# The order of the high and low weight products in the four feed-forwards of a two-block transformer kernel

## The chip, the core and the metric

The kernel runs on one core of one Trainium2 chip. Its time is the device time of one execution, in microseconds (us). The kernel before takes 1095.96 us, the median of three executions from 1095.06 to 1097.74 us.

## What is computed

Two transformer blocks run one behind the other on one sequence of 256 tokens of width 1024, in float32. The first is feed-forward, sparse attention with a pooling branch, feed-forward; the second is feed-forward, a gated mixer, feed-forward. The four feed-forwards are the places that the change is about (the gated mixer is touched as well). Cut to them:

```python
D_MODEL = 1024
SEQ = 256
D_FF = 2816

def swiglu(x, w_gate, w_up, w_down):
    return (jax.nn.silu(x @ w_gate) * (x @ w_up)) @ w_down

x = x + 0.5 * swiglu(rms_norm(x, ffn1_norm[l]), ffn1_w_gate[l], ffn1_w_up[l], ffn1_w_down[l])
...
z = h @ w_in                      # the gated mixer's first projection, width 7168
y_a = spatial_gating(u, v, sgu_norm, sgu_w, sgu_b) @ w_proj_a
y_b = (gate_b * short_conv(gate_c * xb, conv_w)) @ w_proj_b
```

## The kernel before

**Split numbers.** Each float32 operand is held as the sum of a high and a low part in the type fp32r. The activations lie side by side in one tile, `x_hl[:, k, 0, :]` high and `x_hl[:, k, 1, :]` low, 256 tokens each; `hid_hl`, `ya_hl` and `yb_hl` are the same for the hidden features and the mixer's branches. A product of a 128x128 weight tile takes two passes of TensorE into one PSUM bank of 512 columns. The **high pass** (`w_hi` as weights) streams 512 columns, high and low activations at once. The **low pass** (`w_lo` as weights) streams the 256 high columns and is added to the bank's first half. The product of low with low is left out. Each pass loads its own 128x128 weights. A high pass and a low pass of one tile are called a pair below.

**Weights.** They come from memory as blocks of 128x1024, eight 128x128 tiles each, in the order of use, through a ring of four slots (`RING`). SyncE issues the transfers, ScalarE rounds a block into `w_hi` (L429), VectorE subtracts to get `w_lo` (L780) and raises `w_split`. TensorE waits for `w_split` at the first pass of a block and raises `w_used` at its last, which frees the slot.

**A feed-forward** (`ffn(e, n0, p)`, e from 0 to 3) has 66 blocks. `wide_block` takes one block, eight pairs for k = 0 to 7 (`KC`), into one bank. The first two blocks are worked in turn with each other (k outside, two banks), the next two by `wide_block`; then `sum_squares` adds the squares for the norm (L1321); then come 40 blocks, a gate and an up block for each of the 20 remaining chunks of 128 hidden features, the last 32 of them in a hardware loop. For a chunk ScalarE and VectorE make the hidden features, and GpSimd subtracts the high part from them (L347) and raises `hid_split`, once for each of the 22 chunks (`FC`). The down part is 8 output tiles m of 22 pairs k. The weight tile of m and k is number 22m+k in a row of blocks of eight, so the 22 pairs of an m are cut at the ends of blocks: 8, 8 and 6 for m = 0. In m = 0 each k waits for its own chunk (`hid_split`).

**The gated mixer** calls `wide_block` for 56 blocks. The attention mixer does not: it works by `three`, three passes of equal length (L1250 to L1252). No planner sets an order: each engine's program is written out, and semaphores hold the engines together.

Of the kernel before, what the change touches and what calls it, by code (L numbers as in the profile page):

```python
# [26 lines left out]
P = 128  # L27
D = 1024
S = 256
KC = D // P  # L30
TT = S // P
FF = 2816
FC = FF // P
# [13 lines left out]
RING = 4  # L47
# [7 lines left out]
UP_B = 2 * FC  # L55
# [21 lines left out]
def build(nc, stream, x_in, cols_in, rows_in, const_in, sgu_w_in, pool_w_in, out):  # L77
    ctx = ExitStack()
    with ctx:
# [41 lines left out]
        hid_hl, mix_hl, ya_hl, yb_hl = wide[:, 0:FC], wide[:, 0:KC], wide[:, KC:2 * KC], wide[:, 2 * KC:3 * KC]  # L121
# [50 lines left out]
        bank = [pair[i // 2][:, i % 2, :] for i in range(8)]  # L172
# [45 lines left out]
        hid_split = sem("hid_split")  # L218
# [1028 lines left out]
        def _(pe):  # L1247
            def three(dst, a_hi, a_lo, b_hi, b_lo, first, last):
# [2 lines left out]
                nc.tensor.matmul(dst, a_hi, b_lo, start=False, stop=False, skip_group_check=True)  # L1251
                return nc.tensor.matmul(dst, a_lo, b_hi, start=False, stop=last, skip_group_check=True)  # L1252

            def both(dst, a_hi, a_lo, b_hl, first, last):

                nc.tensor.matmul(dst, a_hi, b_hl.rearrange("p a s -> p (a s)"), start=first, stop=False, skip_group_check=True)  # L1256
                return nc.tensor.matmul(dst[:, 0:S], a_lo, b_hl[:, 0, :], start=False, stop=last, skip_group_check=True)  # L1257

            def wide_block(n, dst, b_hl, i=0, per=0):

                slot = n % RING
                pe.wait_ge(w_split, n + 1 + per * i)
                for k in range(KC):
                    w = slice(k * P, (k + 1) * P)
                    last = both(dst[:], w_hi[:, slot, w], w_lo[:, slot, w], b_hl[:, k, :, :], k == 0, k == KC - 1)
                last.then_inc(w_used, 1)

            def feature_block(n, dst, b_hi, b_lo, i=0, per=0, p=None, ready=None):
# [61 lines left out]
            def ffn(e, n0, p):  # L1330

                if p == 0:
                    pe.wait_ge(half_split, 2)
                for k in range(KC):
                    if k == (KC // 2 if p == 0 else 0):
                        pe.wait_ge(w_split, n0 + 2)
                    pe.wait_ge(x_split, 8 * p + k + 1)
                    w = slice(k * P, (k + 1) * P)
                    for c in range(2):
                        slot = (n0 + c) % RING  # L1340
                        last = both(bank[4 + c][:, :], w_hi[:, slot, w], w_lo[:, slot, w], x_hl[:, k, :, :], k == 0, k == KC - 1)
                        if k == KC - 1:
                            last.then_inc(w_used, 1)
                wide_block(n0 + 2, bank[6], x_hl)
                wide_block(n0 + 3, bank[7], x_hl)
                sum_squares(p)

                def chunk(f, j, i=0):

                    wide_block(n0 + 2 * f, bank[2 * j], x_hl, i, 8)  # L1350
                    wide_block(n0 + 2 * f + 1, bank[2 * j + 1], x_hl, i, 8)
# [12 lines left out]
                for m in range(KC):  # L1364
                    if m == 0:
                        pe.wait_ge(parts_added, FC * e + FC - 3)
                    elif m == 2:
                        pe.wait_ge(parts_added, FC * e + FC - 2)
                    elif m >= 4:
                        pe.wait_ge(down_read, KC * e + m - 3)  # L1370
                    for k in range(FC):
                        tile = FC * m + k
                        n, w = n0 + UP_B + tile // KC, slice(tile % KC * P, (tile % KC + 1) * P)
                        if tile % KC == 0:
                            pe.wait_ge(w_split, n + 1)
                        if m == 0:
                            pe.wait_ge(hid_split, FC * e + k + 1)
                        last = both(bank[m % 4][:, :], w_hi[:, n % RING, w], w_lo[:, n % RING, w], hid_hl[:, k, :, :], k == 0,
                                    k == FC - 1)
                        if tile % KC == KC - 1:  # L1380
                            last.then_inc(w_used, 1)
                        elif k == FC - 1:
                            last.then_inc(down_done, 1)

            def attention_mixer(n0, p):
# [202 lines left out]
MIX1_SPLITS = (1, 2, 4, 7, 9)  # L1588

DOWN_LAST = [((m + 1) * FC - 1) // KC for m in range(KC)]  # L1590
DOWN_ENDS = [((m + 1) * FC) % KC == 0 for m in range(KC)]

STAT = [3, 3, 3, 3, 3, 3, 4]
# [109 lines left out]
```

## Time and profile before

| what | us |
|---|---|
| time, median of three executions | 1095.96 |
| the profiled execution's own time | 1094.97 |
| its span in the trace | 1093.2 |
| TensorE busy (share of the span) | 1080.8 (99%) |
| VectorE busy | 783.8 (72%) |
| ScalarE busy | 617.4 (56%) |

The page of the profile gives busy time by engine, then the groups of instructions by line. A TensorE record begins when its pass begins to stream and lasts through the pipeline behind it, so records of passes overlap: a high pass is shown with 396 ns and a low one with 280 ns, while the next begins much sooner. What a pass costs is therefore read from start to start in the timeline. Busy time says only that TensorE was never without work. In the order of time, feed-forward 0 runs from 8 to about 197 us, the attention mixer to 297, feed-forwards 1 and 2 to 481 and 665, the gated mixer to 897, feed-forward 3 to 1081.

### The profile page before, as it was taken

The page shows a single profiled execution, that of the slowest core. Times are in us where ns is not written, and L with a number is a line of the kernel's source. Part 1 is how long each engine was busy: PE and PEld are TensorE (multiplying, and loading weights), DVE is VectorE, ACT ScalarE, POOL GpSimd, SP SyncE. Part 2 cuts the span into 40 slices and gives each one's busy share as a digit, 9 for nine tenths or more (in the row PEclk, how much of TensorE's full clock was granted, in tenths as well). Part 3 has the DMA queues.
Part 4 walks back from the last instruction along what each step waited for, and adds up shares of the span by engine and source line. Part 5 has one row for each costly group of instructions (what it writes and reads, how often), then busy time and mean ns, then how long its engine had stood idle before and what let it go on. Part 6 is the DMA issues. An engine that isn't in the chain of part 4 may idle for free.

```text
span 1093.2 us, 17873 instructions
## 1 busy us (share of the span) xinstructions
PE 1080.8 (99%) x6282; PEld 944.2 (86%) x6282; DVE 783.8 (72%) x1114; ACT 617.4 (56%) x945; POOL 187.8 (17%) x199
## 2 busy tenths in 40 slices
PE   8999999999999999999999999999999999999997
PEld 6888888888988888888888888889988898888886
DVE  6866666797797666668666676787877669666664
ACT  7655544465675555456555545755655557555541
POOL 4411101020031111011111100133201012111100
PEclk9999999999999999999999999999999999999998
DMA  7755555453256555556555554655455545655561
GB/s 280 269 188 189 186 180 175 171 177 134 96 175 210 192 190 176 191 175 209 195 188 188 182 191 155 221 183 192 155 192 182 185 152 203 201 191 190 177 192 39
DMA packets 55571, 200.02 MB, mean 183 GB/s; under 512 B 6304, under 2 KB 6304, under 8 KB 55392
## 3 DMA queue, kind: packets, MB, share of 16 engines
q1 hardware_dynamic: 54576, 196.11, 52.9%
q0 software_dynamic: 512, 2.65, 0.6%
q8 instruction: 33, 0.54, 0.2%
q10 hardware_dynamic: 432, 0.57, 0.2%
q14 instruction: 18, 0.15, 0.0%
HBM read 198.26 MB, written 1.05 MB: 182 GB/s over the span
## 4 chain that ended last, share of the span: by engine, by line
PE 94%; DVE 4%; DMA 1%; ACT 0%; issue 0%; ACTq 0%; DVEq 0%
PE pair L1256 53%; PE pair L1257 27%; PE pair L1250 4%; PE pair L1252 4%; PE pair L1251 4%; DVE w_lo L780 1%; DVE x_hl L786 1%; PE pair L1472 1%; DMA x<-x_in 1%; PE pair L1482 0%; DVE x L797 0%; PE pair L1535 0%; PE pair L1577 0%; PE pair L1493 0%; DVE x_sq L926 0%
## 5 line engine op out<-in xcount | busy, mean ns | idle before, releaser
L780 DVE TENSOR_TENSOR w_lo<-w_raw,w_hi 128x1024 fp32r<-128x1024 f32 x369 | 462.1, 1259 | 226.3 <-ACT w_hi L429 225.9
L1256 PE MATMUL pair<-x_hl,w_hi 128*128 128x512 f32 x1728 | 606.6, 396 | 2.6 <-DVE x_hl L786 1.6
L429 ACT ACTIVATE w_hi<-w_raw 128x1024 fp32r<-128x1024 f32 x369 | 386.4, 1056 | 240.5 <-PE pair L1257 205.2
L1257 PE MATMUL pair<-x_hl,w_lo 128*128 128x256 f32 x1728 | 483.5, 280 | 0.0
L1256 PEld LDWEIGHTS pair<-x_hl,w_hi 128*128 128x128 f32 x1728 | 323.9, 187 | 80.5 <-DVE w_lo L780 2.0
L1257 PEld LDWEIGHTS pair<-x_hl,w_lo 128*128 128x128 f32 x1728 | 326.1, 189 | 0.1
L1256 PE MATMUL pair<-wide,w_hi 128*128 128x512 f32 x832 | 291.0, 394 | 0.0
L1257 PE MATMUL pair<-wide,w_lo 128*128 128x256 f32 x832 | 232.7, 280 | 0.0
L1256 PEld LDWEIGHTS pair<-wide,w_hi 128*128 128x128 f32 x832 | 156.0, 187 | 36.4
L1257 PEld LDWEIGHTS pair<-wide,w_lo 128*128 128x128 f32 x832 | 157.0, 189 | 0.0
L347 POOL TENSOR_TENSOR wide<-side,wide 128x256 fp32r<-128x256 f32 x88 | 86.5, 983 | 375.9 <-ACT wide L491 375.9
L341 POOL TENSOR_TENSOR x_sq<-x_sq 128x256 f32<-128x256 f32 x42 | 39.2, 934 | 269.8 <-ACT x_sq L432 267.8
L436 ACT ACTIVATE x_hl<-x,cols 128x256 fp32r<-128x256 f32 x48 | 22.8, 503 | 76.6 <-DVE x L894 70.3
L846 DVE TENSOR_TENSOR tmp<-pair,side 128x512 f32<-128x512 f32 x88 | 60.2, 684 | 3.5 <-ACT side L483 3.1
L483 ACT ACTIVATE side<-pair 128x512 f32<-128x512 f32 x88 | 51.2, 582 | 5.5 <-PE pair L1257 5.4
L487 ACT ACTIVATE tmp<-tmp 128x256 f32<-128x256 f32 x88 | 35.6, 405 | 15.7 <-DVE tmp L848 15.7
L1250 PE MATMUL pair<-w_hi,x_hl 128*128 128x512 f32 (+1 forms) x112 | 43.5, 389 | 0.5 <-DVE w_lo L780 0.5
L848 DVE TENSOR_TENSOR tmp<-tmp,rstd 128x256 f32<-128x256 f32 x88 | 40.5, 460 | 3.0
L1252 PE MATMUL pair<-w_hi,x_hl 128*128 128x512 f32 (+1 forms) x112 | 42.4, 379 | 0.0
L1251 PE MATMUL pair<-w_lo,x_hl 128*128 128x512 f32 (+1 forms) x112 | 42.4, 378 | 0.0
L855 DVE TENSOR_TENSOR side<-tmp 128x256 f32<-128x256 f32 x88 | 37.2, 423 | 4.8 <-POOL wide L347 2.9
L491 ACT ACTIVATE wide<-side 128x256 f32 (+1 forms) x88 | 36.0, 409 | 7.8 <-DVE side L855 7.8
(185 smaller groups left out, 829.2 us busy)
## 6 DMA issues: line engine op xcount, KB each, us to landing
w_raw<-stream SPq DMA_DIRECT2D x369, 512.0 KB, 4.2
const<-const_in POOLq DMA_DIRECT2D x1, 1248.0 KB, 8.3
w_raw<-stream SPq DMA_DIRECT2D x4, 256.0 KB, 5.7
out<-x_sq SPq DMA_DIRECT2D x4, 256.0 KB, 2.6
rows<-rows_in POOLq DMA_DIRECT2D x1, 576.0 KB, 10.3
x<-x_in ACTq DMA_DIRECT2D x2, 256.0 KB, 5.7
x<-x_in SPq DMA_DIRECT2D x2, 256.0 KB, 7.0
sgu_w<-sgu_w_in POOLq DMA_DIRECT2D x1, 512.0 KB, 13.3
```

The source lines that it names most:

```text
L341: nc.gpsimd.tensor_tensor(x_sq[:, 0, :], x_sq[:, 0, :], x_sq[:, k, :], ALU.add).then_inc(x_sq_added, 1)
L347: nc.gpsimd.tensor_tensor(hid_lo[:, f, :], hid_b[:, f % 2, :], hid_hi[:, f, :].bitcast(F32), ALU.subtract).then_inc(hid_split, 1)
L429: nc.scalar.activation(w_hi[:, slot, :], w_raw[:, slot, :], ACT.Copy).then_inc(w_hi_done, 1)
L483: nc.scalar.activation(low_s[:], pair[j][:, :, S:2 * S], ACT.Copy).then_inc(low_copied, 1)
L780: nc.vector.tensor_tensor(w_lo[:, slot, :], w_raw[:, slot, :], w_hi[:, slot, :].bitcast(F32), ALU.subtract).then_inc(w_split, 1)
L846: nc.vector.tensor_tensor(sum_s, pair[j][:, :, 0:S], low_s[:], ALU.add).then_inc(parts_added, 1)
L848: nc.vector.tensor_tensor(gate_s, gate_s, rstd[:], ALU.mult).then_inc(gate_scaled, 1)
L1250: nc.tensor.matmul(dst, a_hi, b_hi, start=first, stop=False, skip_group_check=True)
L1251: nc.tensor.matmul(dst, a_hi, b_lo, start=False, stop=False, skip_group_check=True)
L1252: return nc.tensor.matmul(dst, a_lo, b_hi, start=False, stop=last, skip_group_check=True)
L1256: nc.tensor.matmul(dst, a_hi, b_hl.rearrange("p a s -> p (a s)"), start=first, stop=False, skip_group_check=True)
L1257: return nc.tensor.matmul(dst[:, 0:S], a_lo, b_hl[:, 0, :], start=False, stop=last, skip_group_check=True)
```

## The change

`both`, the pair of passes, is taken apart into `by_high` and `by_low`, and a function `passes_of` gives the order in which the passes of a run of pairs are issued. The passes are the same, on the same data and into the same banks; the sums in a bank are formed in another order.

- Order 0 (feed-forward 0, and all other calls of `wide_block`: the third and fourth block of each feed-forward and the 56 blocks of the gated mixer): two high, two low passes, and again.
- Order 1 (feed-forward 1): four high, four low.
- Order 2 (feed-forward 2): low, high, low, high.
- Order 3 (feed-forward 3): high passes one pair ahead: high 0, high 1, low 0, high 2, low 1, and so on, two low passes at the end of each run.

In the down part a run is what lies in one block. The wait for `hid_split` in m = 0 now stands once for a run and asks for the run's last chunk. The first two blocks of each feed-forward still go high, low.

```diff
-            def wide_block(n, dst, b_hl, i=0, per=0):
+            def wide_block(n, dst, b_hl, i=0, per=0, order=0):
...
-                for k in range(KC):
-                    w = slice(k * P, (k + 1) * P)
-                    last = both(dst[:], w_hi[:, slot, w], w_lo[:, slot, w], b_hl[:, k, :, :], k == 0, k == KC - 1)
+                passes = passes_of(order, KC)
+                for q, (high, k) in enumerate(passes):
+                    w, ends = slice(k * P, (k + 1) * P), (q == 0, q == len(passes) - 1)
+                    if high:
+                        last = by_high(dst, w_hi[:, slot, w], b_hl[:, k, :, :], *ends)
+                    else:
+                        last = by_low(dst, w_lo[:, slot, w], b_hl[:, k, :, :], *ends)
...
-                    for k in range(FC):
-                        tile = FC * m + k
-                        n, w = n0 + UP_B + tile // KC, slice(tile % KC * P, (tile % KC + 1) * P)
+                    for run in DOWN_RUNS[m]:
+                        tile = FC * m + run[0]
+                        n = n0 + UP_B + tile // KC
                         if tile % KC == 0:
                             pe.wait_ge(w_split, n + 1)
                         if m == 0:
-                            pe.wait_ge(hid_split, FC * e + k + 1)
+                            pe.wait_ge(hid_split, FC * e + run[-1] + 1)
...
+def passes_of(order, n):
+
+    if order == 2:
+        return [(high, k) for k in range(n) for high in (False, True)]
+    if order == 3:
+        high = [(True, k) for k in range(n)]
+        low = [(False, k) for k in range(n)]
+        mixed = [one for two in zip(high[1:], low) for one in two]
+        return high[:1] + mixed + low[-1:]
+    size = (2, 4)[order]
+    return [(high, k) for g in range(0, n, size) for high in (True, False) for k in range(g, min(g + size, n))]
```

TensorE, feed-forward 0, the fifth block, right behind the sum of squares. Before (`x_hl` is the activations, `pair` the PSUM bank):

```order
L1321 MATMUL pair<-x_sq,ones 128x256 [waits x_sq_added]
L1256 MATMUL pair<-x_hl,w_hi 128x512 [waits w_split]
L1257 MATMUL pair<-x_hl,w_lo 128x256
L1256 MATMUL pair<-x_hl,w_hi 128x512
L1257 MATMUL pair<-x_hl,w_lo 128x256
```

The same place in the changed kernel, where `x2` stands for two passes of one kind in a row:

```order
L1334 MATMUL pair<-x_sq,ones 128x256 [waits x_sq_added]
L1256 MATMUL pair<-x_hl,w_hi 128x512 [waits w_split]
L1256 MATMUL pair<-x_hl,w_hi 128x512
L1261 MATMUL pair<-x_hl,w_lo 128x256 x2
L1256 MATMUL pair<-x_hl,w_hi 128x512 x2
L1261 MATMUL pair<-x_hl,w_lo 128x256 x2
```

The long and the short passes stand in twos; the wait for the block stays at its first pass.

TensorE, feed-forward 0, first output tile of the down part, the third run (k = 16 to 21), `wide` being the tile that holds the hidden features. Before:

```order
L1256 MATMUL pair<-wide,w_hi 128x512 [waits hid_split,w_split]
L1257 MATMUL pair<-wide,w_lo 128x256
L1256 MATMUL pair<-wide,w_hi 128x512 [waits hid_split]
L1257 MATMUL pair<-wide,w_lo 128x256
L1256 MATMUL pair<-wide,w_hi 128x512 [waits hid_split]
```

In the changed kernel:

```order
L1256 MATMUL pair<-wide,w_hi 128x512 [waits hid_split,w_split]
L1256 MATMUL pair<-wide,w_hi 128x512
L1261 MATMUL pair<-wide,w_lo 128x256 x2
L1256 MATMUL pair<-wide,w_hi 128x512 x2
L1261 MATMUL pair<-wide,w_lo 128x256 x2
```

Six waits, one for each hidden chunk, have become one in front of the run, for its last chunk.

## Rows read from the trace of the kernel before

**Rows 1.** Page, part 1: busy us (share of the span) and instructions by engine.

```profile
PE 1080.8 (99%) x6282; PEld 944.2 (86%) x6282; DVE 783.8 (72%) x1114; ACT 617.4 (56%) x945; POOL 187.8 (17%) x199
```

**Rows 2.** Page, part 4: the chain that ended last, shares by engine.

```profile
PE 94%; DVE 4%; DMA 1%; ACT 0%; issue 0%; ACTq 0%; DVEq 0%
```

**Rows 3.** Waits of TensorE: who waited for whom, us, times, longest.

```profile
PE pair L1582 <- DVE newton L1235: 1.6, 1, 1.6
PE pair L1256 <- DVE x_hl L786: 1.6, 2, 1.0
```

**Rows 4.** Windows, high passes alone: stretch, its length, busy and passes, granted clock.

```profile
40.00:120.00 80.00, 80.00 (x227) 42.49 (x227) 1.00 0.58 197
320.00:400.00 80.00, 80.00 (x231) 43.12 (x232) 1.00 0.58 196
500.00:580.00 80.00, 80.00 (x232) 43.23 (x232) 1.00 0.57 190
790.00:860.00 70.00, 70.00 (x200) 37.25 (x199) 1.00 0.55 187
930.00:1010.00 80.00, 80.00 (x232) 43.12 (x232) 1.00 0.58 191
```

**Rows 5.** Timeline of TensorE in feed-forward 0: start us, length us, pass.

```profile
99.67 0.40 PE L1256 MATMUL pair<-x_hl,w_hi 128*128 128x512 f32 x1
99.91 0.28 PE L1257 MATMUL pair<-x_hl,w_lo 128*128 128x256 f32 x1
100.02 0.40 PE L1256 MATMUL pair<-x_hl,w_hi 128*128 128x512 f32 x1
...
104.97 0.40 PE L1256 MATMUL pair<-x_hl,w_hi 128*128 128x512 f32 x1
```

**Rows 6.** Timeline of TensorE in feed-forward 1.

```profile
340.06 0.39 PE L1256 MATMUL pair<-x_hl,w_hi 128*128 128x512 f32 x1
340.29 0.28 PE L1257 MATMUL pair<-x_hl,w_lo 128*128 128x256 f32 x1
...
345.26 0.39 PE L1256 MATMUL pair<-x_hl,w_hi 128*128 128x512 f32 x1
```

**Rows 7.** Timeline of TensorE, attention mixer, passes of 512 columns only.

```profile
216.21 0.39 PE L1251 MATMUL pair<-w_lo,x_hl 128*128 128x512 f32 x1
...
218.93 0.39 PE L1251 MATMUL pair<-w_lo,x_hl 128*128 128x512 f32 x1
```

**Rows 8.** Timeline of TensorE, attention mixer, passes of 256 columns only.

```profile
261.89 0.28 PE L1252 MATMUL pair<-wide,w_lo 128*128 128x256 f32 x1
...
263.93 0.28 PE L1251 MATMUL pair<-wide,w_hi 128*128 128x256 f32 x1
```

**Rows 9.** Timeline of TensorE, gated mixer, from 256-column passes into high and low in turn.

```profile
782.84 0.28 PE L1252 MATMUL pair<-x_hl,w_lo 128*128 128x256 f32 x1
782.96 0.40 PE L1256 MATMUL pair<-x_hl,w_hi 128*128 128x512 f32 x1
...
785.08 0.40 PE L1256 MATMUL pair<-x_hl,w_hi 128*128 128x512 f32 x1
```

**Rows 10.** Timeline of TensorE around the sum of squares of feed-forward 1.

```profile
310.40 0.59 PE L1256 MATMUL pair<-x_hl,w_hi 128*128 128x512 f32 x1
310.82 0.28 PE L1257 MATMUL pair<-x_hl,w_lo 128*128 128x256 f32 x1
310.94 0.39 PE L1256 MATMUL pair<-x_hl,w_hi 128*128 128x512 f32 x1
...
311.28 0.39 PE L1256 MATMUL pair<-x_hl,w_hi 128*128 128x512 f32 x1
```

**Rows 11.** Timeline of GpSimd: the last hidden chunk of feed-forward 1.

```profile
425.51 1.47 POOL L347 TENSOR_TENSOR wide<-side,wide 128x256 fp32r<-128x256 f32 x1 [2.07 <-ACT wide L491]
```

**Rows 12.** Timeline of TensorE's weight loads there: the load for k = 16.

```profile
426.96 0.19 PEld L1256 LDWEIGHTS pair<-wide,w_hi 128*128 128x128 f32 x1
```

**Rows 13.** Timeline of TensorE there: the low pass of k = 15, the high pass of k = 16.

```profile
426.95 0.28 PE L1257 MATMUL pair<-wide,w_lo 128*128 128x256 f32 x1
427.07 0.39 PE L1256 MATMUL pair<-wide,w_hi 128*128 128x512 f32 x1
```

**Rows 14.** Timelines of VectorE and TensorE at the third block of feed-forward 0.

```profile
14.11 1.23 DVE L780 TENSOR_TENSOR w_lo<-w_raw,w_hi 128x1024 fp32r<-128x1024 f32 x1
...
15.39 0.50 PE L1256 MATMUL pair<-x_hl,w_hi 128*128 128x512 f32 x1 [0.21 <-DVE w_lo L780]
15.73 0.28 PE L1257 MATMUL pair<-x_hl,w_lo 128*128 128x256 f32 x1
```

More of the change, by code:

```diff
@@ L1252, in three, with by_high, by_low @@
                 return nc.tensor.matmul(dst, a_lo, b_hi, start=False, stop=last, skip_group_check=True)
+            def by_high(dst, a_hi, b_hl, first, last):
+                return nc.tensor.matmul(dst[:, :], a_hi, b_hl.rearrange("p a s -> p (a s)"), start=first, stop=last,
+                                        skip_group_check=True)
+            def by_low(dst, a_lo, b_hl, first, last):
+                return nc.tensor.matmul(dst[:, 0:S], a_lo, b_hl[:, 0, :], start=first, stop=last, skip_group_check=True)
             def both(dst, a_hi, a_lo, b_hl, first, last):
-                nc.tensor.matmul(dst, a_hi, b_hl.rearrange("p a s -> p (a s)"), start=first, stop=False, skip_group_check=True)
-                return nc.tensor.matmul(dst[:, 0:S], a_lo, b_hl[:, 0, :], start=False, stop=last, skip_group_check=True)
-            def wide_block(n, dst, b_hl, i=0, per=0):
+                by_high(dst, a_hi, b_hl, first, False)
+                return by_low(dst, a_lo, b_hl, False, last)
+            def wide_block(n, dst, b_hl, i=0, per=0, order=0):
                 slot = n % RING
                 pe.wait_ge(w_split, n + 1 + per * i)
-                for k in range(KC):
-                    w = slice(k * P, (k + 1) * P)
-                    last = both(dst[:], w_hi[:, slot, w], w_lo[:, slot, w], b_hl[:, k, :, :], k == 0, k == KC - 1)
+                passes = passes_of(order, KC)
[5 more added lines that the diff above has]
+                        last = by_low(dst, w_lo[:, slot, w], b_hl[:, k, :, :], *ends)
                 last.then_inc(w_used, 1)
@@ L1348, in chunk @@
                 def chunk(f, j, i=0):
-                    wide_block(n0 + 2 * f, bank[2 * j], x_hl, i, 8)
-                    wide_block(n0 + 2 * f + 1, bank[2 * j + 1], x_hl, i, 8)
+                    wide_block(n0 + 2 * f, bank[2 * j], x_hl, i, 8, e)
+                    wide_block(n0 + 2 * f + 1, bank[2 * j + 1], x_hl, i, 8, e)
                 for f in range(2, LEAD):
@@ L1376, in ffn @@
                         if m == 0:
-                            pe.wait_ge(hid_split, FC * e + k + 1)
-                        last = both(bank[m % 4][:, :], w_hi[:, n % RING, w], w_lo[:, n % RING, w], hid_hl[:, k, :, :], k == 0,
-                                    k == FC - 1)
-                        if tile % KC == KC - 1:
+                            pe.wait_ge(hid_split, FC * e + run[-1] + 1)
+                        passes = passes_of(e, len(run))
+                        for q, (high, kk) in enumerate(passes):
+                            k = run[kk]
+                            w = slice((FC * m + k) % KC * P, ((FC * m + k) % KC + 1) * P)
+                            ends = (q == 0 and k == 0, q == len(passes) - 1 and k == FC - 1)
+                            if high:
+                                last = by_high(bank[m % 4], w_hi[:, n % RING, w], hid_hl[:, k, :, :], *ends)
+                            else:
+                                last = by_low(bank[m % 4], w_lo[:, n % RING, w], hid_hl[:, k, :, :], *ends)
+                        if (FC * m + run[-1]) % KC == KC - 1:
                             last.then_inc(w_used, 1)
-                        elif k == FC - 1:
+                        elif run[-1] == FC - 1:
                             last.then_inc(down_done, 1)
@@ L1590 @@
 DOWN_LAST = [((m + 1) * FC - 1) // KC for m in range(KC)]
+DOWN_RUNS = [[[k for k in range(FC) if (FC * m + k) // KC == b] for b in range(FC * m // KC, DOWN_LAST[m] + 1)]
+             for m in range(KC)]
+def passes_of(order, n):
[8 more added lines that the diff above has]
+    return [(high, k) for g in range(0, n, size) for high in (True, False) for k in range(g, min(g + size, n))]
 DOWN_ENDS = [((m + 1) * FC) % KC == 0 for m in range(KC)]
```

## Prediction

> **What bounds the kernel now.** I read the page's busy times first. TensorE is busy for 1080.8 of 1093.2 us, VectorE for 72% [rows 1], and the chain that ended last is TensorE for 94% [rows 2]. The longest waits of TensorE in the whole run are of 1.6 us [rows 3], in places that the change does not touch. So the time is the sum of TensorE's passes, and a change of their order counts only if it changes the distance from one start to the next, or makes a pass wait.
>
> The record lengths do not give that distance, the timeline does. In feed-forward 0 a pair (one high, one low pass) takes (104.97 - 99.67) / 15 = 0.3533 us: 0.24 from the high start to the low one, 0.12 to the next high one [rows 5]. In feed-forward 1 the same 15 pairs take 5.20 us, 0.3467 each [rows 6]. Code, shapes and granted clock (1.00) are the same. The windows of high passes alone show that each rhythm lasts: 227 high passes in 80 us of feed-forward 0, 231 and 232 in 80 us of feed-forwards 1, 2 and 3, and 200 in 70 us of the gated mixer, which is the slow rhythm again [rows 4] (the counts include a pass cut by either edge). One sequence of passes thus has **two steady rhythms**, 6.7 ns a pair apart, and the kernel stays in one until something disturbs TensorE.
>
> The Trainium skill ("TensorE: Matmul & The Clock Gate", Back-to-back issue gap) gives N/2.4 + 2.5 ns for a pass alone, so 216 and 109 ns, 325 a pair. Neither rhythm agrees: 347 and 353 ns were measured, so no saving down to 325 is counted.
>
> What do passes of one length cost? Twelve passes of 512 columns take 2.72 us, 0.2267 each [rows 7]; 17 passes of 256 columns take 2.04 us, 0.1200 each [rows 8]. Their sum is 0.3467 us, just the fast rhythm. I take that as the price without disturbance, and the 6.7 ns as an extra that only a change between lengths brings.
>
> **Feed-forward 0 and the gated mixer, order 0.** Of feed-forward 0, all but the first 16 pairs, 512, come from the third block on and run in the slow rhythm: 512 x 6.67 ns = 3.4 us above the fast one. The gated mixer has 56 x 8 = 448 pairs: 3.0 us. Together 6.4 us are to be had. Bounds of the grouped order: if twos run like passes of one length, all 6.4 is saved; if the extra stays with every pair, nothing. In between, the extra belongs to a high pass that follows a low one, and of these there is one in two pairs instead of one in one: half of it goes, 3.2 us. I take the half. The rows show no high pass behind a high pass inside such a mix, and the nearest ones, [rows 5] and [rows 7], are the two ends.
>
> **Feed-forward 1, order 1.** It now runs fast, so it has nothing to win. If fours carry the extra at each change from low to high, that is a quarter: 496 pairs x 6.67 / 4 = 0.8 us added; bounds 0 and 3.3. I take 0.8, by the same reasoning as above.
>
> **Feed-forward 2, order 2.** Low, high, low, high is the same alternation as before with the ends of the runs shifted by one pass. In the steady state nothing changes. Zero, with bounds 0 and 512 x 6.67 = 3.4 us if the rhythm happens to fall the other way.
>
> **Feed-forward 3, order 3.** Seven of eight neighbours still alternate; two high passes open and two low ones close each run. I take zero, bounds 0 and 496 x 6.67 = 3.3 us.
>
> **The wait for the hidden chunks.** In m = 0 the third run starts 16 pairs into the down part and now asks for chunk 21 instead of chunk 16. GpSimd ends that chunk at 425.51 + 1.47 = 426.98 us [rows 11]; the weight load of k = 16, which carries the wait, starts at 426.96 [rows 12], with the low pass of k = 15 at 426.95, and its own pass at 427.07 [rows 13]. So the load comes 0.02 us too early. From the end of a VectorE step to the pass that waited for it 15.39 - (14.11 + 1.23) = 0.05 us go by [rows 14]. The load would start at about 427.03, 0.07 late. What is queued behind it on TensorE are all other passes; VectorE and ScalarE wait for TensorE's slots, not the other way round, so this 0.07 us is on the path. The other feed-forwards stand alike to within 0.1 us. The lower bound is 0, where the last up blocks run slower than now; the upper one is 0.07 + 0.10, since a pass behind a late start comes 0.34 instead of 0.24 us later [rows 14], [rows 5]. Four times 0.07 to 0.1: **0.3 us**, bounds 0 and 0.7. What the diff does with `w_split`, `w_used` and `down_done` stands at the same pass ends as before and costs nothing: VectorE, at 72%, is the cover [rows 1].
>
> **Sum** on the profiled execution (1094.97 us, 1.8 above its span and 1.0 below the median): -1.7 (feed-forward 0) - 1.5 (gated mixer) + 0.8 + 0 + 0 + 0.3 = -2.1 us. On the median, 1095.96 - 2.1 = **1093.9 us**.
>
> **Rivals.**
> - **Grouping frees the passes entirely.** Twos and fours cost 0.3467 a pair: -3.4 - 3.0 + 0.3 = -6.1, 1089.9 us. For it speaks that the two one-length rows add up to the fast rhythm exactly; against it, that twos change length as often as every second pass.
> - **Every entry into a mix falls into the slow rhythm** (the other side). Where 256-column passes end and high and low begin, six pairs take 785.08 - 782.96 = 2.12 us, 0.3533 each, from the first [rows 9]; behind the sum of squares, a pass of another kind, the rhythm becomes fast (310.94 to 311.28 [rows 10]). If two equal passes in a row are such an entry, order 3 makes one in every block and feed-forward 3 goes slow, +3.3; the late load in m = 0 may do it to the last 160 pairs of feed-forward 2, +1.1. With the sum above: -2.1 + 4.4 = +2.3, 1098.3 us. If also the twos and fours keep the whole extra, it is 3.3 (feed-forward 1) + 3.3 + 1.1 + 0.3 = +8.0, 1104.0 us. It decides from the point where equal passes come at least once in a block.
> - **Order does nothing.** A weight load starts with the pass before its own (426.96 beside 426.95 [rows 12, 13]), one ahead, whatever the kinds are; the rhythm is then set by how TensorE was last disturbed, as before, and only the waits are added: +0.3, 1096.3 us. The Trainium skill (same page, section LDWEIGHTS) gives P/1.2 ns for a load, 107 for 128 columns, an estimate that is below every distance in the trace; by that rule loads are hidden under either pass in any order, which is this case. The trace agrees as far as no pass is shorter than 0.12 us.
>
> **How the numbers follow.** The forecast has a chance of 0.36, full freedom 0.19, the entry case 0.15 at 1098.3 and 0.07 at 1104.0, no effect 0.23. A measurement of this kernel can tell about 0.3%, 3.3 us, from no change: faster means below 1092.7, slower above 1099.2. Faster gets the 0.19 and a third of the forecast, whose own range, from half to all of one stretch's extra, is 1091.5 to 1096: 0.31. Slower gets the 0.07 and the upper half of the entry case, plus some of the rest, where the rhythm of feed-forwards 2 and 3 falls the other way: 0.19. Same: 0.50. The range reaches from the full freedom (1089.9, less 0.9 for the spread of the runs) to 1099.5; it leaves out the worst entry case and little else.
>
> **What would show it.** In the trace of the changed kernel, two pairs of order 0 (four passes) take 0.700 us in the forecast, 0.693 with full freedom, 0.707 with no gain; four pairs of order 1 take 1.393, 1.387 or 1.413. Starts in feed-forwards 2 and 3 show 0.347 or 0.353 a pair directly. The load of k = 16 in each m = 0 should stand about 0.05 us behind the end of GpSimd's last chunk, and TensorE should show no other new wait. The forecast is wrong if a high pass behind a high one costs other than 0.227 us or a low one behind a low one other than 0.120, since every number above rests on these two.

## The result and the profile after

The changed kernel takes 1096.16 us (median of 22 executions, 1095.58 to 1097.53), the kernel before 1094.57 us (22 executions, 1091.14 to 1098.66). The ratio is 1.0022, with a 95% interval from 1.0012 to 1.0032: slower by 0.22%, which is less than the 0.3% that the prediction called no change. The forecast was 1093.9 us, a change of -2.1 us from its median of three executions. Measured was +1.6 us; the sign is wrong.

The spreads differ as well. The executions of the kernel before lie in levels: 6 from 1091.1 to 1091.9, one at 1092.4, 12 from 1094.3 to 1096.0 and 3 from 1097.5 to 1098.7. The changed kernel has one, 1.9 us wide. Such levels make the median of the kernel before a matter of the draw: the executions of it that were measured beside the experiments below have medians from 1091.97 to 1094.95 us. The changed kernel lies above all of them.

The page of the changed kernel says again that TensorE is the bound: busy for 1081.2 us, where [rows 1] had 1080.8, of a span now 0.9 us longer.

```profile
span 1094.1 us, 17873 instructions
PE 1081.2 (99%) x6282; PEld 944.0 (86%) x6282; DVE 783.4 (72%) x1114; ACT 617.7 (56%) x945; POOL 186.7 (17%) x199
```

Where the 0.9 us comes from is read at five marks in the timeline of TensorE: the sum of squares, which stands right behind the fourth block of each feed-forward, and in the gated mixer (that of the attention mixer is left out). Then the last group of passes. The kernel before:

```profile
21.15 0.38 PE L1321 MATMUL pair<-x_sq,ones 128*128 128x256 f32 x1
...
310.15 0.38 PE L1321 MATMUL pair<-x_sq,ones 128*128 128x256 f32 x1
...
493.63 0.38 PE L1321 MATMUL pair<-x_sq,ones 128*128 128x256 f32 x1
...
676.92 0.38 PE L1321 MATMUL pair<-x_sq,ones 128*128 128x256 f32 x1
...
908.73 0.38 PE L1321 MATMUL pair<-x_sq,ones 128*128 128x256 f32 x1
...
1086.33 1.22 PE L1582 MATMUL pair<-newton,ones 128*128 128x128 f32 x4 [1.60 <-DVE newton L1235]
```

The changed kernel at the same marks:

```profile
20.81 0.38 PE L1334 MATMUL pair<-x_sq,ones 128*128 128x256 f32 x1
...
307.32 0.38 PE L1334 MATMUL pair<-x_sq,ones 128*128 128x256 f32 x1
...
492.86 0.38 PE L1334 MATMUL pair<-x_sq,ones 128*128 128x256 f32 x1
...
677.33 0.38 PE L1334 MATMUL pair<-x_sq,ones 128*128 128x256 f32 x1
...
906.83 0.38 PE L1334 MATMUL pair<-x_sq,ones 128*128 128x256 f32 x1
...
1087.23 1.22 PE L1602 MATMUL pair<-newton,ones 128*128 128x128 f32 x4 [1.60 <-DVE newton L1235]
```

| stretch, mark to mark | order | before | changed | difference | forecast |
|---|---|---|---|---|---|
| start to 1 | first blocks of feed-forward 0 | 21.15 | 20.81 | -0.3 | |
| 1 to 2 | 0, rest of feed-forward 0, attention | 289.00 | 286.51 | -2.5 | -1.7 |
| 2 to 3 | 1, feed-forward 1 | 183.48 | 185.54 | +2.1 | +0.8 |
| 3 to 4 | 2, feed-forward 2 | 183.29 | 184.47 | +1.2 | 0 |
| 4 to 5 | 0, gated mixer | 231.81 | 229.50 | -2.3 | -1.5 |
| 5 to end | 3, feed-forward 3 | 177.60 | 180.40 | +2.8 | 0 |

(The forecast's 0.3 for the waits is spread over four of the rows. Most of the first row is one wait of the first two blocks, whose order did not change: its pass starts 1.28 us behind the one before it in the kernel before, 1.03 us in the changed one.) The starts give the price of a pair. Twos, feed-forward 0 of the changed kernel, 20 pairs in 67.23 - 60.26 = 6.97 us, **0.3485** us each (0.3483 over the 80 us from 40 to 120), between the two rhythms of [rows 5] (0.3533) and [rows 6] (0.3467); two passes in a row are merged into one line here:

```profile
60.26 0.63 PE L1256 MATMUL pair<-x_hl,w_hi 128*128 128x512 f32 x2
...
67.23 0.62 PE L1256 MATMUL pair<-x_hl,w_hi 128*128 128x512 f32 x2
```

Fours, feed-forward 1, 16 pairs in 345.63 - 340.01 = 5.62 us, **0.351** each (0.3508 over longer stretches):

```profile
340.01 1.09 PE L1256 MATMUL pair<-x_hl,w_hi 128*128 128x512 f32 x4
340.94 0.64 PE L1261 MATMUL pair<-x_hl,w_lo 128*128 128x256 f32 x4
...
345.63 0.63 PE L1256 MATMUL pair<-x_hl,w_hi 128*128 128x512 f32 x2
```

One high ahead, feed-forward 3, a block of eight pairs in 932.56 - 929.74 = 2.82 us, **0.3525** each:

```profile
929.74 0.63 PE L1256 MATMUL pair<-x_hl,w_hi 128*128 128x512 f32 x2
...
932.56 0.63 PE L1256 MATMUL pair<-x_hl,w_hi 128*128 128x512 f32 x2
```

Feed-forward 2 has both rhythms. It runs at 0.3467 us a pair until the first output tile of the down part. There GpSimd's last chunk ends at 608.22 + 1.48 = 609.70. The first weight load of k = 16, that of the low pass, starts at 609.81. That is 0.37 behind the load before it, where 0.12 is usual for a load of `w_lo` (the row of `fine_waits` below), so the load is 0.25 us late. The passes lose less by it: two pairs from 609.55 on take 610.38 - 609.55 = 0.83 us instead of 0.69, 0.14 more. From there four pairs take 611.80 - 610.38 = 1.42 us, 0.355 each by these two decimals. Timelines of GpSimd, of weight loads and of TensorE:

```profile
608.22 1.48 POOL L347 TENSOR_TENSOR wide<-side,wide 128x256 fp32r<-128x256 f32 x1 [2.06 <-ACT wide L491]
```

```profile
609.44 0.19 PEld L1256 LDWEIGHTS pair<-wide,w_hi 128*128 128x128 f32 x1
609.81 0.19 PEld L1261 LDWEIGHTS pair<-wide,w_lo 128*128 128x128 f32 x1 [0.19 <-issue]
```

```profile
609.55 0.39 PE L1256 MATMUL pair<-wide,w_hi 128*128 128x512 f32 x1
609.84 0.36 PE L1261 MATMUL pair<-wide,w_lo 128*128 128x256 f32 x1
...
610.38 0.40 PE L1256 MATMUL pair<-wide,w_hi 128*128 128x512 f32 x1
...
611.80 0.40 PE L1256 MATMUL pair<-wide,w_hi 128*128 128x512 f32 x1
```

The windows of high passes alone count the same over longer stretches (columns as in [rows 4]): 100 us of feed-forward 2's up part hold 290, 40 us of its down part 114, 80 us of feed-forward 3 229.

```profile
500.00:600.00 100.00, 100.00 (x290) 53.93 (x289) 1.00 0.57 190
620.00:660.00 40.00, 40.00 (x114) 21.24 (x114) 1.00 0.57 184
...
930.00:1010.00 80.00, 77.92 (x229) 40.70 (x227) 1.00 0.57 186
```

With these prices the rows from the second on add up. Feed-forward 0: 512 x (0.3533 - 0.3483) = 2.6 us less; mixer: 448 x 0.0050 = 2.2 less; feed-forward 1: 496 x (0.3508 - 0.3467) = 2.0 more; feed-forward 2: 160 x 0.0067 = 1.1 and a wait of 0.1 more; feed-forward 3: 496 x 0.0058 = 2.9 more.

### The profile page after: what moved, and what is told of

It reads as the page before. It is cut to its first block, busy times and chain, and to the rows that moved or that the text cites. A ratio compares the mean times of both kernels' runs of the same rounds, so it can differ in the third digit from the quotient of the medians.

```text
span 1094.1 us, 17873 instructions
## 1 busy us (share of the span) xinstructions
PE 1081.2 (99%) x6282; PEld 944.0 (86%) x6282; DVE 783.4 (72%) x1114; ACT 617.7 (56%) x945; POOL 186.7 (17%) x199
## 4 chain that ended last, share of the span: by engine, by line
PE 94%; DVE 4%; DMA 1%; ACT 0%; issue 0%; ACTq 0%; DVEq 0%
PE pair L1256 53%; PE pair L1261 27%; PE pair L1250 4%; PE pair L1251 4%; PE pair L1252 4%; DVE w_lo L780 1%; DVE x_hl L786 1%; PE pair L1492 1%; DMA x<-x_in 1%; PE pair L1502 0%; DVE x L797 0%; PE pair L1555 0%; PE pair L1597 0%; PE pair L1513 0%; DVE x_sq L926 0%
## 5 line engine op out<-in xcount | busy, mean ns | idle before, releaser
L1256 PE MATMUL pair<-x_hl,w_hi 128*128 128x512 f32 x1728 | 553.3, 396 | 3.1 <-DVE x_hl L786 2.1
L1261 PE MATMUL pair<-x_hl,w_lo 128*128 128x256 f32 x1728 | 380.2, 280 | 0.0
L1261 PEld LDWEIGHTS pair<-x_hl,w_lo 128*128 128x128 f32 x1728 | 314.3, 188 | 41.8
L1256 PEld LDWEIGHTS pair<-x_hl,w_hi 128*128 128x128 f32 x1728 | 291.4, 188 | 39.6 <-issue 2.8
L1256 PE MATMUL pair<-wide,w_hi 128*128 128x512 f32 x832 | 266.4, 396 | 0.0
L1261 PE MATMUL pair<-wide,w_lo 128*128 128x256 f32 x832 | 182.6, 280 | 0.0
L1261 PEld LDWEIGHTS pair<-wide,w_lo 128*128 128x128 f32 x832 | 151.1, 188 | 20.4 <-issue 0.2
L1256 PEld LDWEIGHTS pair<-wide,w_hi 128*128 128x128 f32 x832 | 140.2, 188 | 17.2
```

What stands on the lines that cost most here:

```text
L1256: return nc.tensor.matmul(dst[:, :], a_hi, b_hl.rearrange("p a s -> p (a s)"), start=first, stop=last, skip_group_check=True)
```

## Experiments: is it the order or the place?

Each kernel below is the changed one with an edit, of which the lines that matter are shown. `ORDERS` gives the order of each feed-forward in place of `e`. `twos_all` gives all feed-forwards order 0.

```diff
+ORDERS = (0, 0, 0, 0)
-                        passes = passes_of(e, len(run))
+                        passes = passes_of(ORDERS[e], len(run))
```

(and the same in the calls of `wide_block`, here and in all kernels below that have `ORDERS`.)

> The changed kernel with order 0 (two high, two low) in all four feed-forwards. Theory A, each order has a price of its own: twos cost 0.3483 us a pair in feed-forward 0 and in the gated mixer of the changed kernel, so they cost that in every feed-forward. Against the changed kernel that is 496 x (0.3508 - 0.3483) = 1.2 us less in feed-forward 1, +0.5 - 0.8 in feed-forward 2 and 496 x (0.3525 - 0.3483) = 2.1 us less in feed-forward 3: about 1092.5 us, with little spread from run to run. Theory B, the place and the way in decide and the order does not: feed-forwards 1 and 3 keep their 0.3508 and 0.3525 and the time stays at 1096.

Measured: 1092.83 us (12 executions, 1092.51 to 1093.78), 0.9983 of the kernel before (0.9967 to 0.9999). 230 or 231 high passes in 80 us of feed-forwards 0, 1 and 3 alike, of which the first and the last are shown:

```profile
40.00:120.00 80.00, 72.05 (x231) 35.01 (x230) 1.00 0.60 197
...
930.00:1010.00 80.00, 72.14 (x230) 34.93 (x230) 1.00 0.55 190
```

`rotated` gives each order to the next place.

```diff
+ORDERS = (1, 2, 3, 0)
-                        passes = passes_of(e, len(run))
+                        passes = passes_of(ORDERS[e], len(run))
```

> The changed kernel with each order in another place: feed-forward 0 in fours, 1 low first in turn, 2 one high ahead, 3 in twos. Theory A, each order has a price of its own: 0.3508 us a pair in feed-forward 0, 0.3525 in 2, 0.3483 in 3, and feed-forward 1 at 0.3467 or 0.3533 (in turn has two rhythms). Sum of the four about as in the changed kernel, 1094 to 1098 us. Theory B, the place decides: feed-forward 0 stays at 0.3483, 1 at 0.3508, 2 at 0.3467, 3 at 0.3525.

Measured: 1095.99 us (10 executions, 1095.80 to 1097.06). The fours have moved to feed-forward 0 with their 229 passes in 80 us, the high-ahead order to feed-forward 2, the low-first order to feed-forward 1. That one runs fast in the up part (231) and slow in the down part (143 in 50 us; the fast rhythm has 145), as it did in the other place:

```profile
40.00:120.00 80.00, 62.19 (x229) 38.85 (x228) 1.00 0.59 197
320.00:400.00 80.00, 80.00 (x231) 43.12 (x232) 1.00 0.60 197
430.00:480.00 50.00, 50.00 (x143) 26.61 (x142) 1.00 0.55 188
```

Both kernels say theory A: **an order has a price of its own**, wherever it stands. Grouped orders have one price; in turn has two.

## Experiments: the wait at k = 16

`fine_waits` undoes one part of the change: in m = 0 each k waits for its own chunk.

```diff
-                        if m == 0:
-                            pe.wait_ge(hid_split, FC * e + run[-1] + 1)
...
+                            if m == 0 and kk not in [one for _, one in passes[:q]]:
+                                pe.wait_ge(hid_split, FC * e + k + 1)
```

> The changed kernel with one part undone: in the first output tile of the down part each k waits for its own hidden chunk again. Theory A, the late weight load at k = 16 throws feed-forward 2 from the fast rhythm (0.3467 us a pair) into the slow one (0.3533) for the rest of its down part: with it gone all of feed-forward 2 stays fast, 160 x 6.67 ns = 1.1 us, and with the four waits of 0.08 us the time is 1.4 us less, 1094.8 us. Theory B, the wait costs only what it waits, and the slow rhythm there has another cause: 0.3 us less, 1095.9 us, and the down part of feed-forward 2 stays slow.

Measured: 1094.99 us (12 executions, 1094.35 to 1095.69), 1.2 us under the changed kernel. The same 40 us of feed-forward 2's down part now hold 116 high passes instead of 114:

```profile
620.00:660.00 40.00, 40.00 (x116) 21.51 (x116) 1.00 0.58 186
```

The load that was late there starts 0.12 behind the one before it here (timeline of weight loads):

```profile
609.42 0.19 PEld L1256 LDWEIGHTS pair<-wide,w_hi 128*128 128x128 f32 x1
609.54 0.19 PEld L1261 LDWEIGHTS pair<-wide,w_lo 128*128 128x128 f32 x1
```

`in_turn_coarse` does that part alone: high, low in turn everywhere as before, and the one wait for a run.

```diff
-            def wide_block(n, dst, b_hl, i=0, per=0, order=0):
+            def wide_block(n, dst, b_hl, i=0, per=0, order=6):
...
+ORDERS = (6, 6, 6, 6)        # high, low in turn, as in the kernel before
...
-    size = (2, 4)[order]
+    size = {0: 2, 1: 4, 4: 8, 5: 3, 6: 1}[order]
```

> The kernel before (high, low in turn everywhere) with one part of the change alone: in the first output tile of the down part one wait for each run of pairs, for its last chunk. Theory A, a late weight load draws the rhythm anew: some or all of the down parts behind k = 16 of feed-forwards 1, 2 and 3 run at 0.3533 us a pair instead of 0.3467, up to 3 x 160 x 6.67 ns = 3.2 us, plus 0.3 us of waiting: between 1095 and 1098 us against 1094.6. Theory B, it costs only what it waits: 0.3 us more than the kernel before.

Measured: 1097.20 us (12 executions, 1094.0 to 1099.5), 1.0019 of the kernel before (1.0001 to 1.0037). In its profiled execution the weight load of k = 16 is late in every feed-forward. Behind it feed-forwards 0, 1 and 2 run slow (140 in 49 us, 143 in 50, 114 in 40); only feed-forward 3 stays fast (131 in 45). Ahead of it, the up part of feed-forward 0 issues the same passes as in the kernel before, and here it ran fast: 232 high passes in 80 us, against 227 in [rows 4]. So one and the same stretch can fall into either rhythm in two executions.

```profile
40.00:120.00 80.00, 80.00 (x232) 43.15 (x231) 1.00 0.58 198
141.00:190.00 49.00, 49.00 (x140) 26.00 (x140) 1.00 0.57 188
...
430.00:480.00 50.00, 50.00 (x143) 26.55 (x142) 1.00 0.56 188
...
620.00:660.00 40.00, 40.00 (x114) 21.25 (x114) 1.00 0.56 184
...
1030.00:1075.00 45.00, 45.00 (x131) 24.24 (x130) 1.00 0.51 161
```

So the wait is worth about 0.1 us where it stands and 1.1 us more where it throws an in-turn stretch of 160 pairs from the fast rhythm into the slow one. That was theory A of both, and it holds, though not every late load does it: in feed-forward 3 the load is late by the same 0.15 us as in the others. The 1097.20 us are a median over many draws of the rhythm; the profiled execution took 1095.59.

## Experiments: how the extra depends on the grouping

```diff
+ORDERS = (4, 5, 7, 2)        # eights; threes; twos, low ones first; low first in turn
```

> The changed kernel with other groupings, and with the wait for each hidden chunk at its own k: feed-forward 0 in eights (eight high, eight low), 1 in threes (3, 3 and 2), 2 in twos with the low ones first, 3 low and high in turn; the gated mixer stays in twos. Theory A, the extra grows with the run of equal passes (in turn, fast, 32 array cycles a pass over the columns, twos 34, fours 37): eights cost 0.3508 us a pair or more, threes lie between, about 0.350. Theory B, the extra comes with each change of length and dies away along a run: eights cost less than fours, near 0.3467 to 0.349. Twos with the low ones first should cost 0.3483 as the others in both; low and high in turn 0.3467 or 0.3533.

Measured: 1092.68 us (one execution), span 1090.9. Eights, feed-forward 0, 32 pairs in 91.35 - 80.18 = 11.17 us, 0.349 each:

```profile
80.18 2.00 PE L1256 MATMUL pair<-x_hl,w_hi 128*128 128x512 f32 x8
82.02 1.11 PE L1261 MATMUL pair<-x_hl,w_lo 128*128 128x256 f32 x8
...
91.35 0.86 PE L1256 MATMUL pair<-x_hl,w_hi 128*128 128x512 f32 x3
```

Threes, feed-forward 1: a block of 3, 3 and 2 pairs takes 342.92 - 340.13 = 2.79 us, 0.349 each by these decimals.

```profile
340.13 0.86 PE L1256 MATMUL pair<-x_hl,w_hi 128*128 128x512 f32 x3
...
342.92 0.86 PE L1256 MATMUL pair<-x_hl,w_hi 128*128 128x512 f32 x3
```

Neither theory holds alone. The extra over 0.3467 us a pair is 1.7 ns in twos, 2.9 in threes, 4.1 in fours, and falls again to 2.5 in eights. For a whole group that is 3 ns in twos, 17 in fours and 20 in eights. A group of two pairs is cheap, one of four costs about as much as one of eight.

The starts in the traces say where the extra lies. Below are the mean distances from a pass of one kind to the next pass, in ns, each over a stretch of 80 us (`before`, `after` and `sizes`; the last row from [rows 7, 8]).

| order | high to high | high to low | low to low | low to high | a pair |
|---|---|---|---|---|---|
| in turn, fast | | 230.0 | | 116.7 | 346.7 |
| in turn, slow | | 236.0 | | 117.3 | 353.3 |
| twos | 233.0 | 233.3 | 114.6 | 115.8 | 348.3 |
| fours | 233.6 | 228.3 | 118.6 | 118.3 | 350.8 |
| eights | 230.6 | 226.7 | 118.9 | 120.1 | 349.2 |
| one length only | 226.7 | | 120.0 | | |

On average, in every mix a high pass costs more than the 226.7 ns that it costs among its like, and a low pass costs less than its 120.0. So even the fast rhythm is no sum of undisturbed passes: there a high pass costs 3.3 ns more and a low one 3.3 less, and the two cancel. In twos a high pass costs the same behind a high one as behind a low one. The extra of the high passes is smaller in eights (230.1 on average) than in fours (232.3), so it does die away along a run, but slowly. Twos with the low ones first (feed-forward 2) cost what the others do, and low first in turn (feed-forward 3) ran fast from end to end, 232 in 80 us. What in TensorE makes these distances was not found.

## Experiments: what leads into the fast rhythm

In turn is the cheapest order if it runs fast. `nudges` keeps the kernel before and puts an extra pass in front of each chunk, of another kind in each feed-forward.

```diff
+                    if e < 3:
+                        nudge(bank[2 * j], e)        # in front of each chunk
...
+            def nudge(dst, kind=0):
+                if kind == 0:
+                    nc.tensor.matmul(dst[:, 0:S], ones[:], ones[:].unsqueeze(1).to_broadcast([P, 2, P]), start=True, stop=True, skip_group_check=True)
+                elif kind == 1:
+                    nc.tensor.matmul(dst[:, 0:1], ones[:], ones[:, 0:1], start=True, stop=True, skip_group_check=True)
+                else:
+                    nc.tensor.matmul(dst[:, 0:S], zeros[:, 0:P], zeros[:, 0:S], start=True, stop=True, skip_group_check=True)
```

> The kernel before, its order and waits, with one extra pass in front of every chunk of hidden features, 20 in a feed-forward: in feed-forward 0 a float32 pass of 256 columns like the sum of squares, in 1 a float32 pass of one column, in 2 a bf16 pass of 256 columns, none in 3; and the 256-column float32 pass in front of each of the gated mixer's two stretches of high and low passes. All write into a bank that the next pass begins anew. Its time says little, the extra passes cost some 15 us. Theory A, a float32 pass is an entry that leads into the fast rhythm (in the traces so far behind 7 of 8 sums of squares, where in-turn passes follow): behind nearly all of the 20 in feed-forward 0, and both in the mixer, a pair takes 0.3467 us. Theory B, each disturbance draws the rhythm by chance: about as many stretches at 0.3533 as at 0.3467, in all kinds alike.

Measured: 1114.49 us (one execution). Behind the float32 passes of 256 columns the chunks run slow, slow, fast, in this order and over again, 6 fast of 20. Three chunks in a row, high passes 14 pairs apart: 33.61 - 28.66 = 4.95 us, 39.60 - 34.75 = 4.85, 45.67 - 40.72 = 4.95:

```profile
28.66 0.40 PE L1256 MATMUL pair<-x_hl,w_hi 128*128 128x512 f32 x1
...
33.61 0.40 PE L1256 MATMUL pair<-x_hl,w_hi 128*128 128x512 f32 x1
...
34.75 0.39 PE L1256 MATMUL pair<-x_hl,w_hi 128*128 128x512 f32 x1
...
39.60 0.39 PE L1256 MATMUL pair<-x_hl,w_hi 128*128 128x512 f32 x1
...
40.72 0.40 PE L1256 MATMUL pair<-x_hl,w_hi 128*128 128x512 f32 x1
...
45.67 0.40 PE L1256 MATMUL pair<-x_hl,w_hi 128*128 128x512 f32 x1
```

Behind the 20 float32 passes of one column and the 20 bf16 passes all chunks run slow. The mixer's two stretches, with one such float32 pass each, both ran fast, as theory A had it. But with 6 of 20 in feed-forward 0 theory A falls: such a pass leads nowhere for sure. It is no chance draw either, since the 20 repeat with a period of three. The reading that fits is that the rhythm follows from the exact moment at which the first passes start; no run sets that moment by itself, so this is argued and not shown.

`re_entered` has the kernel before with three of the 256-column passes.

```diff
+                nudge(bank[0])        # in front of each of the mixer's two stretches
...
+                        if e == 0:
+                            nudge(bank[2 * ((f + 2) % 4)])
```

> The kernel before with three extra float32 passes of 256 columns, one in front of each of the gated mixer's two stretches of high and low passes and one in front of the gate block of chunk 3 in feed-forward 0. Theory A, such a pass leads into the fast rhythm: the mixer's 448 pairs run at 0.3467 instead of 0.3533 us, 3.0 us less, feed-forward 0 nearly always too, and each extra pass costs about 0.3: the median falls from 1094.7 to about 1089, and the three levels of the kernel before (1091, 1094.5, 1098) become mostly one. Theory B, the rhythm is drawn by chance: no clear change of the median, +0.9 us, and the levels stay.

Measured: 1093.28 us (12 executions, 1089.3 to 1096.8), ratio 1.0006 (0.9988 to 1.0023). The profiled execution had the mixer and nearly all of feed-forward 0 fast (204 high passes in 70 us of the mixer against 200 in [rows 4]) and took 1089.4. Only 3 of the 12 lie below 1091; 6 lie from 1092.6 to 1094.0 and 3 above 1096, too long for a program that is fast everywhere. The kernel before, measured beside it, had a median of 1091.97 us (17 executions, 9 of them in its lowest level), so the medians here tell little. No gain to rely on: theory B.

```profile
790.00:860.00 70.00, 70.00 (x204) 37.75 (x203) 1.00 0.60 193
```

In all four traces that have it so far, low first behind twos and the sum of squares had come out fast in the up part (feed-forward 1 of `rotated`, 2 of the changed kernel and of `fine_waits`, 3 of `sizes`). `low_first` puts this way in into all four feed-forwards.

```diff
+ORDERS = (2, 2, 2, 2)        # and each k waits for its own chunk, as in fine_waits
```

> All four feed-forwards low first in turn (order 2), the wait for each hidden chunk at its own k, the third and fourth block of each feed-forward and the mixer in twos as in the changed kernel. Theory A, the entry decides: twos, then the sum of squares, then low first led into the fast rhythm in all four traces that have it (feed-forward 2 of the changed kernel and two more, feed-forward 1 of the rotated one), and will in each feed-forward. Against all twos (1092.8 us) that is 4 x 496 x 1.67 ns = 3.3 us less and 0.3 less for the waits: 1089.2 us, in one narrow level. Theory B, low and high in turn draws its rhythm by chance: 3.3 us more for each feed-forward that falls slow, 1091 to 1097 us, in levels.

Measured: **1089.18 us** (12 executions, 1088.74 to 1092.18), 0.9944 of the kernel before (0.9926 to 0.9962). It beats both kernels, and the median is the one that theory A gave, but the one narrow level is not there. Eight executions lie from 1088.7 to 1089.4 and four from 1091.6 to 1092.2. The profiled one is of the upper level, and its windows show which part is slow: feed-forward 0 (227 in 80 us), and no other. So this entry led into the fast rhythm in three of the four feed-forwards.

```profile
40.00:120.00 80.00, 80.00 (x227) 42.47 (x227) 1.00 0.61 197
320.00:400.00 80.00, 80.00 (x232) 43.18 (x231) 1.00 0.60 196
...
930.00:1010.00 80.00, 80.00 (x232) 43.14 (x231) 1.00 0.58 190
```

Where the gain comes from is seen level against level. The lowest level of `low_first` is at 1089.0 us, that of the kernel before, measured beside it, at 1091.1. The 2.2 us between them fit what the mixer's twos save (448 x 5.0 ns = 2.2 us). The rest of the 5.8 us between the medians comes from how often a higher level is drawn: 8 of 12 executions of `low_first` lie in the lowest level and none near 1098, against 9 (up to 1092.5) and 11 (above 1097.4) of 29 of the kernel before.

`high_first` changes the first pass of each pair only.

```diff
-ORDERS = (2, 2, 2, 2)        # as in low_first
+ORDERS = (6, 6, 6, 6)        # high, low in turn
```

> As low_first, but high first in turn behind the sum of squares, as in the kernel before; the third and fourth block of each feed-forward and the mixer stay in twos. Theory A1, the twos in front of the sum of squares fix the entry: fast everywhere, one narrow level at 1089.2 us. Theory A2, the low pass behind the sum of squares does it: with the high pass there the rhythm falls in levels 3.3 us apart, between 1089 and 1097 us.

Measured: 1089.86 us (10 executions, 1088.8 to 1092.8), 0.9954 (0.9932 to 0.9976), six at the lower level and four at the upper. Neither sub-theory is clean, but the gain does not hang on the low pass: with twos ahead of the sum of squares, feed-forwards 1 to 3 came out fast in the one profile of each. They did so in the kernel before too [rows 4], with no twos there, so what the twos in front do for the entry is not shown; for them speaks that none of these 22 executions lies near 1098.

`low_first_mixer` also runs the mixer's 448 pairs low first in turn, entered from passes of one length.

```diff
-            def wide_block(n, dst, b_hl, i=0, per=0, order=0):
+            def wide_block(n, dst, b_hl, i=0, per=0, order=2):
...
-                wide_block(n0 + 2, bank[6], x_hl)
-                wide_block(n0 + 3, bank[7], x_hl)
+                wide_block(n0 + 2, bank[6], x_hl, order=7)        # 7: twos, as order 0
+                wide_block(n0 + 3, bank[7], x_hl, order=7)
```

> As low_first, with the gated mixer's 448 pairs low first in turn too, entered straight from passes of one length. Theory A, the entry decides, and that entry led into the slow rhythm each time for high first: the mixer goes from 0.3483 to 0.3533 us a pair, 448 x 5 ns = 2.2 us more than low_first. Rival: with a low pass in front the entry from 256-column passes is no change of length at all, and the rhythm is the fast one: 0.7 us less than low_first.

Measured: 1094.02 us (10 executions, 1091.2 to 1095.6). The mixer is slow, 199 high passes in 70 us. The kernel's four fastest executions (1091.2 to 1091.5) against the lowest level of `low_first` give 1091.2 - 1089.0 = 2.2 us, as theory A has it. The rival falls: entered from passes of one length, in turn came out slow whichever pass was first, in each trace that has this entry. Here twos are better.

```profile
790.00:860.00 70.00, 70.00 (x199) 37.23 (x199) 1.00 0.58 188
```

`first_in_twos` asks whether feed-forward 0 alone makes the two levels.

```diff
-ORDERS = (2, 2, 2, 2)        # as in low_first
+ORDERS = (0, 2, 2, 2)
```

> As low_first, with feed-forward 0 in twos (order 0). In low_first 8 of 12 executions lie at 1089.0 us and 4 at 1091.9, and the profiled one, of the higher level, has feed-forward 0 alone in the slow rhythm. Theory A, only feed-forward 0 draws its rhythm there, as its entry depends on when the first transfers land: in twos it costs 496 x 1.67 ns = 0.8 us more than fast and 2.5 less than slow, always: one level at 1089.9 us. Theory B, another part of the program draws too: two levels about 3 us apart stay.

Measured: 1090.62 us (7 executions, 1089.50 to 1091.16), 0.9969 (0.9955 to 0.9982). The level at 1092 is gone, which supports theory A; the median is 0.7 above the 1089.9 expected, and with 7 executions 1.7 us apart a smaller second draw is not excluded. It is steadier than `low_first`, not faster.

## Why the prediction was wrong

- **What bounds the kernel, and the two rhythms** were read rightly. Every difference between the kernels is a distance from start to start, and the 6.7 ns a pair returned in each experiment. What I missed is that the rhythm can differ from one execution to the next. The one profile had feed-forward 0 slow; 6 of the 22 executions lie a whole level lower, which fits a fast feed-forward 0 (512 x 6.67 ns = 3.4 us). No such execution of this kernel was profiled, but `in_turn_coarse` shows the up part fast. Which part makes the upper level of 1098 is not known. The sum was made against one draw, and its starting point, a median of three, lay 1.4 us above the median of 22. That the fast rhythm is the price without disturbance fails as well: it has a high pass at 230.0 and a low one at 116.7 ns, not 226.7 and 120.0, and only the sum agrees.
- **Order 0** was under-sized. The step was that the extra belongs to a high pass behind a low one, so that half of it goes. Twos cost 0.3483 us a pair, three quarters of it gone: -2.5 and -2.3 us where -1.7 and -1.5 stood.
- **Order 1** was mis-sized the other way, by the same step. A quarter of the extra, 0.8 us, was expected; a pair in fours costs 0.3508, +2.0 us. The rule behind both numbers, so much for each change of length, is false: the extra grows from twos to fours. The sentence on what would make the forecast wrong named it, a high pass behind a high one at other than 0.227 us or a low one behind a low one at other than 0.120. In twos they cost 0.233 and 0.115.
- **Order 3** at zero is the step that turned the sign. It held that seven of eight neighbours still alternate and so nothing changes. The pair costs 0.3525, almost the slow rhythm: +2.9 us. The entry rival had said this, +3.3, because order 3 makes two equal passes in every block.
- **Order 2**: zero for the up part holds (290 in 100 us). The down part went slow for 160 pairs behind the late load, +1.1, again as the entry rival had it; `fine_waits` gives it back.
- **The wait** was sized rightly as a sum, in part by luck. By the starts in the trace the late loads cost the passes 0.14 us in feed-forward 2 and 0.04 to 0.10 in each of the others, 0.36 together, where 0.3 stood. But the load starts 0.11 us behind the end of GpSimd's chunk, not 0.05, and in feed-forward 2 it is 0.25 us late, not 0.07; about half of that the passes do not feel.
- **The entry rival's sum** was 1098.3 us, with order 0 at half price; with order 0's real price it would have been 1.5 lower, near the 1096.2 measured. That it comes so near is in part luck, since it has the fours 1.2 too low and starts from the high median of three. Nor does its rule hold as it stands, that every entry is slow: 6 of the 20 chunks in `nudges` and the last stretch of `in_turn_coarse` ran fast. I gave it 0.15, since only [rows 9] spoke for it. That row and the two steady prices [rows 7, 8] were of equal weight; I built the sum on the latter alone.
- **The rival that order does nothing** falls with `rotated`. The Trainium skill's rule behind it ("TensorE: Matmul & The Clock Gate", LDWEIGHTS: P/1.2 ns for P columns, an estimate of 107 ns for 128) does not settle it: no high or low pass of this kernel or the changed one starts less than 0.11 us before the next, so loads fit by it, and the order still moves a pair by up to 6.7 ns. (The prediction's "no pass is shorter than 0.12 us" is a reading of one length only; in turn some low passes stand 0.112 us apart from the next in the trace of before. And 107 ns is below the distances of high and low passes, not below every distance in that trace.)

## What to carry to other kernels

Where TensorE is never idle, count its starts over tens of passes before and after any change of order, since busy time and record lengths hide several ns a pass, and read more than one execution, since a rhythm can be drawn anew each time. A mix of long and short passes with fresh weights can have a fast and a slow rhythm: pick the order and the way in for each stretch by measurement (here twos behind passes of one length, strict alternation behind twos and a float32 pass). That gave 0.56% with no work removed; of its 5.8 us, 2.2 stand between the lowest levels and the rest is a better draw. Keep waits fine in front of a pass that runs without slack: a late load that held the passes up by 0.14 us cost 1.1 us more in the passes behind it.

## What the runs showed of the hardware

- Passes of 512 and of 256 fp32r columns, each with its own weights, start 0.2267 and 0.1200 us apart in rows of one length [rows 7, 8]; in turn a pair costs 0.3467 or 0.3533, in twos 0.3483, in fours 0.3508, in eights 0.349. In the mixes high passes cost 0.230 to 0.236 us on average, low ones 0.115 to 0.119. The granted clock was 1.00 in all of these stretches.
- The rhythm of passes in turn lasts for hundreds of passes (232 high passes in 80 us) until TensorE is disturbed. What sets it at the entry is not shown: 20 equal entries in one execution came out slow, slow, fast, over and over, and the up part of feed-forward 0 ran slow in one execution (227 in 80 us) and fast in another (232).
- A wait in front of a pass is carried by its weight load, which starts with the pass before. So it has to be met one pass earlier than the data are used, 0.12 to 0.23 us here. A load that waited for GpSimd started 0.11 us behind the end of GpSimd's instruction.
